# Carrying the first softmax's denominator into the head norm's epsilon in a hybrid attention layer

## The reference

```
z1, z2 = scores of (q1, k1) and (q2, k2), scaled, causal
p1, p2 = softmax(z1), softmax(z2)
w  = p1 - lam * p2
yb = w @ v                                             # per head, 128 wide
yb = yb * rsqrt(mean(yb^2) + 1e-5) * subln_gain * (1 - lam_init)
```

## Time and profile before

| | us |
|---|---|
| median of 3 runs | 1628.64 |
| lowest, highest of them | 1626.85, 1629.61 |
| the profiled execution's own time | 1625.79 |
| its span, first to last instruction | 1623.9 |

### The profile page before, as it was taken

One profiled execution on the slowest core, in us unless ns is written; L12 is line 12 of the kernel. 1 busy time (PEld: TensorE's weight loads), 2 busy tenths in 40 slices (PEclk: granted clock), 3 DMA queues, 4 the chain that ended last, 5 costly groups with the idle time before them and its releaser, 6 DMA issues.

```text
span 1623.9 us, 20971 instructions
## 1 busy us (share of the span) xinstructions
PE 1560.0 (96%) x7472; PEld 1291.9 (80%) x7472; DVE 980.0 (60%) x1536; ACT 493.3 (30%) x898; POOL 464.3 (29%) x264
## 2 busy tenths in 40 slices
PE   8999999999989888899999999999999999999996
PEld 6788888878867777787878888888888888888885
DVE  3787878878786776843467644444444444434548
ACT  2454555555555554420222211110111111111111
POOL 2544444444332222102300222222122222212322
PEclk9999999999999999999999999999999999999998
DMA  4111112121110000203521311111111111111102
GB/s 165 53 35 58 52 53 77 39 65 30 50 52 20 21 26 13 65 14 117 182 91 52 117 52 52 52 46 34 51 52 52 52 52 38 39 52 52 52 1 104
DMA packets 98669, 92.44 MB, mean 57 GB/s; under 512 B 3632, under 2 KB 85552, under 8 KB 98480
## 3 DMA queue, kind: packets, MB, share of 16 engines
q1 hardware_dynamic: 98608, 91.63, 17.4%
HBM read 81.13 MB, written 10.49 MB: 56 GB/s over the span
## 4 chain that ended last, share of the span: by engine, by line
PE 76%; DVE 9%; issue 9%; POOL 3%; DMA 2%; ACT 1%; SPq 0%; POOLq 0%; DVEq 0%; ACTq 0%
PE p_z L889 6%; PE p_z L888 6%; PE p_z L887 6%; PE p_proj L541 6%; PE p_proj L545 6%; PE p_proj L543 6%; PE p_proj L865 3%; PE p_proj L866 3%; PE p_proj L867 3%; PE p_tr L640 2%; PE p_av L654 2%; PE p_z L808 2%; PE p_z L810 2%; PE p_z L809 2%; PE p_av L867 2%
## 5 line engine op out<-in xcount | busy, mean ns | idle before, releaser
L541 PE MATMUL p_proj<-xt_h,w_hi 128*128 128x512 f32 x640 | 255.4, 399 | 0.8 <-DVE xt_l L1245 0.8
L545 PE MATMUL p_proj<-xt_h,w_lo 128*128 128x512 f32 x640 | 255.0, 398 | 0.0
L543 PE MATMUL p_proj<-xt_l,w_hi 128*128 128x512 f32 x640 | 252.5, 395 | 0.0
L1639 DVE TENSOR_TENSOR res<-p_z,res 128x512 f32<-128x512 f32 x224 | 150.8, 688 | 109.8 <-PE p_z L889 109.8
L1710 POOL TENSOR_TENSOR w_lo<-w_raw,w_hi 128x1024 fp32r<-128x1024 f32 x48 | 120.9, 2520 | 249.0 <-DVE w_hi L1252 248.5
L1799 POOL TENSOR_TENSOR w_l<-w_raw,w_h 128x1024 fp32r<-128x1024 f32 x31 | 79.5, 2585 | 364.5 <-DVE w_h L1607 364.5
L887 PE MATMUL p_z<-w_h,h_h 128*128 128x512 f32 x448 | 174.3, 389 | 0.0
L888 PE MATMUL p_z<-w_l,h_h 128*128 128x512 f32 x448 | 174.3, 389 | 0.0
L889 PE MATMUL p_z<-w_h,h_l 128*128 128x512 f32 x448 | 174.3, 389 | 0.0
L1216 ACT ACTIVATE relu<-p_proj 128x512 f32<-128x512 f32 x30 | 18.0, 599 | 406.7 <-PE p_proj L867 406.7
L545 PEld LDWEIGHTS p_proj<-xt_h,w_lo 128*128 128x128 f32 x640 | 121.5, 190 | 24.1
(11 more groups left out here) (274 smaller groups left out, 3258.2 us busy)
## 6 DMA issues: line engine op xcount, KB each, us to landing
w_raw<-w_ff SPq DMA_DIRECT2D x64, 512.0 KB, 4.0
w_raw<-w_in SPq DMA_DIRECT2D x40, 512.0 KB, 3.8
gate_rows<-gst SPq DMA_DIRECT2D x12, 512.0 KB, 4.9
y<-x SPq DMA_DIRECT2D x8, 512.0 KB, 9.2
wo_raw<-w_out SPq DMA_DIRECT2D x8, 512.0 KB, 8.7
rows<-x SPq DMA_DIRECT2D x8, 512.0 KB, 3.3
out<-rows_out SPq DMA_DIRECT2D x8, 512.0 KB, 2.6
gst<-gate_rows SPq DMA_DIRECT2D x6, 512.0 KB, 4.2
```

The costliest lines, as they stand in the source:

```text
L541: pe.matmul(o, w_hi[n_slot][:, k, :], xt_h[:, k, cols], start=(k == 0), stop=False)
L543: pe.matmul(o, w_hi[n_slot][:, k, :], xt_l[:, k, cols], start=False, stop=False)
L545: mm = pe.matmul(o, w_lo[n_slot][:, k, :], xt_h[:, k, cols], start=False, stop=(k == KT - 1))
L1639: dve.tensor_tensor(o, by_block(dn_banks[n % 4]), o, ALU.add).then_inc(dn_added, 1)
```

## The change

With `s1`, `s2` the two row sums, the kernel before forms `w = e1/s1 - (lam/s2) * e2`. After the change it forms `s1 * w = e1 - (lam * s1/s2) * e2`. The per-head norm that follows removes a factor of each row, if its epsilon is multiplied by `s1^2`; so each (head, block) gets an epsilon column of its own.

- The reciprocal (L1364) is of one column instead of two.
- The coefficient is `s1 * (1/s2) * (-lam)`: one `tensor_scalar` whose input is a 128x1 tile and whose two scalars are per-partition columns. It replaces the product of two tiles, L1365.
- The scaling of `e2` (L1367, 32 instructions) is gone. The last step has `e2` as first input, the coefficient as its scalar and `e1` as second input; it has the shape of L1368 and still two tiles as inputs.
- Behind it, each unit writes `EPS * s1 * s1` into a column of `eps_rows`: a `tensor_scalar` of 128x1 with two per-partition scalars, counted on VectorE's own semaphore but not waited for on the spot. In groups 5 and 6 the column's address comes from the loop's register.
- At the end `rs_v` is a `scalar_tensor_tensor` with `eps_rows` (128x32) as second input, behind a wait for all of them.

```
+        eps_rows = vecs[:, 208:240]
...
                     dve.wait_ge(z_read, G.z(2 * u + 1) + 1)
-                    own.link(dve.reciprocal(e_inv[s], e_sum[s]))
-                    own.link(dve.tensor_tensor(c_neg[s][:, 0:1], e_inv[s][:, 1:2], n_lam, ALU.mult))
+                    own.link(dve.reciprocal(e_inv[s][:, 1:2], e_sum[s][:, 1:2]))
+                    own.link(dve.tensor_scalar(c_neg[s][:, 0:1], e_sum[s][:, 0:1], e_inv[s][:, 1:2], n_lam,
+                                               ALU.mult, ALU.mult))
                     e1, e2 = df_e1[u % 3], df_e2[u % 3]
-                    own.link(dve.tensor_scalar(e2[:, 0:w], e2[:, 0:w], c_neg[s][:, 0:1], None, ALU.mult))
-                    dve.scalar_tensor_tensor(out=e1[:, 0:w], in0=e1[:, 0:w], scalar=e_inv[s][:, 0:1],
-                                             in1=e2[:, 0:w], op0=ALU.mult, op1=ALU.add).then_inc(a_ready, 1)
+                    dve.scalar_tensor_tensor(out=e1[:, 0:w], in0=e2[:, 0:w], scalar=c_neg[s][:, 0:1],
+                                             in1=e1[:, 0:w], op0=ALU.mult, op1=ALU.add).then_inc(a_ready, 1)
+                    at_u = slice(8 * (g - 4) + u, 8 * (g - 4) + u + 1) if isinstance(g, int) else \
+                        bass.ds(g * 8 + (u - 32), 1)
+                    own(dve.tensor_scalar(eps_rows[:, at_u], e_sum[s][:, 0:1], e_sum[s][:, 0:1], EPS,
+                                          ALU.mult, ALU.mult))
...
-            dve.tensor_scalar(rs_v, p_z[1][:, 0:32], 1.0 / P, EPS, ALU.mult, ALU.add).then_inc(v_eps, 1)
+            own.sync()
+            dve.scalar_tensor_tensor(out=rs_v, in0=p_z[1][:, 0:32], scalar=1.0 / P, in1=eps_rows,
+                                     op0=ALU.mult, op1=ALU.add).then_inc(v_eps, 1)
```

## The result

The changed kernel takes 1609.68 us (1609.36 to 1611.16, 4 runs) against 1628.38 us: a ratio of 0.9887, 95% interval 0.987 to 0.9905. It is 18.7 us faster. The profiled execution went from 1625.79 to 1609.89 us, 15.9 us less.

A forecast was written before the change was run, and what follows sets the result against it. TensorE, busy 1560.0 of 1623.9 us, was taken as the bound, with time won only where it idles or clocks low. Gains of 8.85 us (groups 4 to 6) and 1.82 (group 7) gave 10.7: forecast 1618.0 us, range 1611.5 to 1622.5.

The forecast's parts named there:

- where the hold goes: At units 3 and 6, GpSimd's hold of VectorE passes from L1365 to the last step, which takes over 2 us.
- B: TensorE's wait at unit 6's turn in groups 4 to 7, 3.97 us in group 5; gain 0.93 us each.
- The rival that it goes with L1365: The hold on VectorE is L1365's own and goes altogether: 20 to 28 us gained, near 1605; chance 0.04.
- the one that the coefficient product is held too: GpSimd holds the product replacing L1365, the last step comes behind it: gain 7.1 us, time 1621.5; chance 0.09.
- A: TensorE's wait at unit 3's turn, 1.72 us in group 5; gain 0.98 us, in group 7 only 0.89.
- C: TensorE's wait at unit 7's turn, groups 4 to 6: vanishes, gain 1.04 us; a wait there would show the forecast wrong.
- the small costs: At unit 2, the coefficient product costs 0.06 us more than L1365 and the epsilon write 0.15 us.
- the clock is kept: Rival: no fall to half speed behind unit 6's wait in all three groups, 6 us more, 1612; chance 0.17.
- The price of a fall: In the rival with more falls of TensorE's clock, each fall costs 3.4 us.
- the slower rival: Shifted waits bring more clock falls; the fourth new one makes it slower by more than 0.2%, about 1632; chance 0.04.
- a term at nothing: Removing L1367 in the other units frees VectorE where TensorE does not wait for it; costed at nothing.
- the median carried over: The median of the runs was put 2.85 us above the profiled execution, forecast at 1615.1 us.

The follow-up runs named there:

- product_form_only: The kernel before with only L1365 changed, to one tile times a per-partition scalar; scaling and last step stay: ratio 0.9971, 4.7 us faster.
- two_tile_product: The changed kernel, but with the coefficient as one operation reading two 128x1 tiles and a scalar: 1617.24 us, ratio 0.9933 to the kernel before.
- no_eps_columns: The changed kernel without the 32 epsilon writes, the norm's epsilon left unscaled: 1608.49 us, ratio 0.9887 to the kernel before.

## Why the prediction was wrong

**Right: where the hold goes.** The hold passed from L1365 to the last step (2.96 us at B), as the earlier trace rows had let one infer, and product_form_only and two_tile_product showed it at two other instructions. The rival that it goes with L1365 is out, and so is the one that the coefficient product is held too: it took 0.27 or 0.28 us in all 32 places, somewhat over the 0.16 to 0.22 named as the sign.

**Right: the waits.** The sum had 10.7 us; the trace has 9.9. B gave 0.98 in each of the four groups where the sum had 0.93. A gave 0.83 in group 5 where it had 0.98, but VectorE's part of it came as reckoned. From unit 2's reciprocal to the end of unit 3's last step it is 527.01 - 518.69 = 8.32 us before (the earlier trace rows have the last step) and 520.41 - 513.08 = 7.33 us after, 0.99 less. The other 0.16 us came at TensorE's transposes of unit 2, which had waited that long without a row for it, so TensorE comes to A 0.16 us sooner. First the kernel before, then the changed one:

```profile
518.69 0.16 DVE L1364 RECIPROCAL vecs<-vecs 128x2 f32<-128x2 f32 x1
```

```profile
513.08 0.16 DVE L1365 RECIPROCAL vecs<-vecs 128x1 f32<-128x1 f32 x1
...
518.09 2.32 DVE L1369 SCALAR_TENSOR_TENSOR be<-om,vecs,be 128x512 f32<-128x512 f32 x1 [0.18 <-DVE vecs L1366]
```

C went in groups 4 and 5, its last step in front of the second `k_lo` half; in group 6, where the clock was kept, 0.57 us of it stayed. A wait at C was one of the prediction's signs of being wrong.

**Right: the small costs.** The epsilon writes cost 0.12 us of wait at A and nothing that can be measured in total (1608.49 against 1609.5).

**Wrong: the clock.** The step that failed is "The fall came 2.4 us after the wait had begun (547.87), so I let it stand". It made the half-speed stretches a constant of both kernels, as if a fall came at a fixed time into a wait and lasted 6.8 us. The traces have falls from 1.9 to 5.0 us after the wait began, and they last 3.4 us where they come near its end or behind it. At a B of 3.0 us or less there were 6.8, 6.8 and 3.4 us at half speed in three groups together in the changed kernel's three traces, where both traces of the kernel before have 20.5 us. The rival "the clock is kept", which had 0.17, came nearer: for a group with the clock kept the forecast has 0.98 + 0.93 + 1.04 + 2.0 = 4.95 us, and group 6, the one without a fall, became 5.2 us shorter. That the 2.0 us fit is partly luck. They were 3.4 us of clock less 1.4 us of new wait at C; it was 2.6 less 0.57. Groups 4 and 5 with half the stretch won 4.7 and 4.4, more than the 2.95 forecast. What time at half speed costs with the waits unchanged is shown by the one execution of no_eps_columns that fell three times for 6.8 us and took 6 us more than its siblings.

The price of a fall was off too: 3.4 us was taken for 6.8 us at half speed, but in group 5 the fall came at 550.26 and the wait ended at 551.83, so only the 5.25 us up to 557.08 cost matmuls, 2.6 us. A slip of the sums stands beside it: four new falls of 3.4 us less 10.7 are 2.9 us slower, not more than the 3.3 us that the slower rival names.

**Wrong: a term at nothing.** "L1367's removal in the other units (128, 256, 640, 768 and group 7's 1024 columns) frees VectorE where TensorE does not wait for it" doesn't hold for unit 4, the 640 columns. In the kernel before its transposes come 0.46 us after the filler matmul in front of them, where filler matmuls follow each other at 0.23 us, and VectorE's last step had ended at 532.76:

```profile
532.44 0.39 PE L541 MATMUL p_proj<-xt_h,w_hi 128*128 128x512 f32 x1
532.90 0.55 PE L640 MATMUL p_tr<-small,be 128*128 128x128 f32 x3
```

TensorE does wait here; the rows show it only as a late start. In the changed kernel these transposes come 0.21 to 0.27 us sooner after what is in front of them, 0.7 us over groups 4 to 6. The turn of unit 7 gives 0.2 us more than its wait in groups 4 and 5.

**Wrong: the median carried over.** The forecast put the changed kernel's median 2.85 us over its profiled execution, as in the kernel before. It is 0.2 us under it. Of the 8.3 us between forecast and median 3.1 lie here, the other 5.2 in the profiled execution (1615.1 against 1609.89).

**How the 18.7 us come together.** In the two profiled executions: 9.9 us of waits; 4.8 us less lost to half speed in groups 4 to 6 (15.9 us of matmuls ran at half speed there before, 6.2 after); 1.5 us of the short waits at units 2, 4 and 7; less 1.7 us for the longer stretch behind group 7; and 0.95 us of spread ahead of group 4. That makes 15.4 of their 15.9 us. The rest of the 18.7 is that the profiled execution of the kernel before was 2.6 us under its median: its runs reach from 1623.1 to 1631.5 us over all sessions, those of the changed kernel from 1608.4 to 1612.2. That the slow end of the former is in part more time at half speed shows in the mean clock on record for 48 of its runs: the 19 with 0.986 or 0.987 have a median of 1628.6 us, the 17 with 0.989 or more one of 1626.1. A mean clock lower by 0.003 is, by estimate, 10 us more at half speed over 1625 us. The two don't go together in every run, and the changed kernel's runs, at 0.990 to 0.993, show no such order.

**Open.** Why the fall comes early in the wait in one execution, behind its end in the next, and in a third not at all, is not settled. The changed program itself shows 3.4 us and none at the same B; the 6.8 us at a B of 3.0 us were seen only without the epsilon columns, in the one execution of four whose clock was low. That the program has no part in it is not shown either, since both traces of the kernel before have 20.5 us.

## What to carry to other kernels

A wait of some microseconds on TensorE has two prices, its own length and the matmuls at half speed behind it. When an edit shortens such a wait, the case with the clock kept belongs in the forecast with a weight of its own, not at its edge. When VectorE is held by GpSimd and the held instruction is made one that isn't, the hold goes to the next: here to one with two tiles (2.96 us instead of 1.15), or to a scaling of 896 columns (2.59 instead of 0.69). So look at what VectorE did just before, since the copy that sets GpSimd going may be moved behind the step that TensorE waits for. Here that order was worth as much as the arithmetic, and the two together 25 us.

## What the runs showed of the hardware

- A `tensor_scalar` on a single element in each partition took 0.21 us with one column scalar and 0.27 us with two, against 0.15 with immediates, and was never held by GpSimd's subtraction in these traces; with 896 columns it was (2.59 instead of 0.69 us).
- Between 430 us and the last microseconds of the span, the stretches at half speed lasted 3.4, 6.8 or 10.2 us in every trace. Of the 30 at a wait of TensorE, the 13 whose fall came 0.77 to 1.80 us before the wait's end lasted 6.8 us, the 17 whose fall came later 3.4 us. The same wait of 2.7 or 3.0 us had a fall in one execution of the changed kernel and none in the next.
- A `scalar_tensor_tensor` already held when the first `k_lo` half ended went in front of the second half each time in the changed kernel. In product_form_only the scaling was the held one, and the last step, coming 0.03 us behind it, was held again (3.29 us).
